# Orders of the two residuals and of the first mixer's last context state

## The reference, cut to what matters

```python
# first block
h_lat = modulate(rms_norm(lat, norm_g[i, 0]), mod_l[:, 0], mod_l[:, 1])
y_lat, y_ctx = gla_mixer(h_lat, h_ctx, ...)      # the context is scanned first, its state starts the scan of the tokens
lat = lat + (mod_l[:, 2] * rms_norm(y_lat, norm_g[i, 1])).astype(lat.dtype)              # first residual
h = modulate(rms_norm(lat, norm_g[i, 2]), mod_l[:, 3], mod_l[:, 4])
lat = lat + (mod_l[:, 5] * rms_norm(swiglu(h, ffn_w_in[i], ffn_w_out[i]), norm_g[i, 3])).astype(lat.dtype)  # second residual
# second block
h = h + 0.5 * swiglu_2(rmsnorm(h, ffn1_norm[l]), ffn1_w1[l], ffn1_w3[l], ffn1_w2[l])
```

## Time and profile before

| | us |
|---|---|
| median of 3 runs | 1572.92 (1571.53 to 1576.04) |
| profiled execution, its own time | 1573.41 |
| span of the profiled execution | 1571.6 |
| PE busy | 1554.9 (99% of the span) |
| PE weight loads busy | 1401.0 (89%) |
| DVE busy | 1099.0 (70%) |
| ACT busy | 669.4 (43%) |
| POOL busy | 118.8 (8%) |

### The profile page before, as it was taken

One profiled execution on the slowest core, in us unless ns is written; L12 is line 12 of the kernel. 1 busy time (PEld: TensorE's weight loads), 2 busy tenths in 40 slices (PEclk: granted clock), 3 DMA queues, 4 the chain that ended last, 5 costly groups with the idle time before them and its releaser, 6 DMA issues.

```text
span 1571.6 us, 23036 instructions
## 1 busy us (share of the span) xinstructions
PE 1554.9 (99%) x9758; PEld 1401.0 (89%) x9758; DVE 1099.0 (70%) x1264; ACT 669.4 (43%) x848; POOL 118.8 (8%) x106
## 2 busy tenths in 40 slices
PE   9999999999999999999999999999999999999998
PEld 7888888889999899889899889888988898998997
DVE  5898755688668567699667648646447886785675
ACT  4554275445445425445435425321223452452541
POOL 0100000020000000000000000354006000000000
PEclk9999999999999999999999999999999999999999
DMA  9544510222322322313323322333212222232231
GB/s 386 197 172 161 214 54 28 83 75 85 108 81 108 134 81 108 108 56 106 104 85 108 120 94 79 138 121 107 81 54 81 81 94 94 108 113 103 108 108 54
DMA packets 35878, 172.05 MB, mean 109 GB/s; under 512 B 3008, under 2 KB 5312, under 8 KB 26176
## 3 DMA queue, kind: packets, MB, share of 16 engines
q1 hardware_dynamic: 31424, 153.80, 27.4%
q0 software_dynamic: 4352, 16.78, 3.1%
HBM read 168.47 MB, written 2.10 MB: 109 GB/s over the span
## 4 chain that ended last, share of the span: by engine, by line
PE 82%; DVE 10%; DMA 3%; issue 2%; ACT 2%; POOL 0%; DVEq 0%; POOLq 0%; ACTq 0%; SPq 0%
PE bank L588 81%; DMA raw_pair<-in_ffn_in 3%; DVE form_slot L2548 3%; DVE sum_form L2542 1%; DVE raw_pair L2542 1%; DVE both L2495 1%; ACT form_slot L1738 1%; DVE x_form L2522 0%; DVE qd L2013 0%; DVE xT L2384 0%; ACT w_all L1407 0%; DVE hs L2506 0%; DVE y_ffn L2381 0%; DVE a_lo L2432 0%; DVE w_all L1935 0%
## 5 line engine op out<-in xcount | busy, mean ns | idle before, releaser
L588 PE MATMUL bank<-x_form,form_slot 128*128 128x256 f32 x4536 | 547.7, 283 | 3.4 <-ACT snap_a L1745 1.9
L588 PEld LDWEIGHTS bank<-x_form,form_slot 128*128 128x128 f32 x4536 | 545.9, 192 | 5.6 <-ACT snap_a L1745 2.5
L588 PE MATMUL bank<-g_slot,unit_slot 128*128 128x512 f32 (+1 forms) x1614 | 361.4, 385 | 0.0
L588 PEld LDWEIGHTS bank<-g_slot,unit_slot 128*128 128x128 f32 x1614 | 298.6, 188 | 60.1
L1738 ACT ACTIVATE form_slot<-raw_pair 128x1024 fp32r<-128x1024 f32 x135 | 140.4, 1054 | 235.2 <-PE bank L588 123.9
L588 PE MATMUL bank<-a_hi,w_all 128*128 128x512 f32 x768 | 233.8, 393 | 1.6 <-ACT a_hi L1848 0.9
L2548 DVE TENSOR_TENSOR form_slot<-raw_pair,form_slot 128x1024 fp32r<-128x1024 f32 x135 | 164.1, 1221 | 73.3 <-ACT form_slot L1738 73.2
L588 PEld LDWEIGHTS bank<-a_hi,w_all 128*128 128x128 f32 x768 | 143.1, 188 | 34.0 <-issue 3.8
L588 PE MATMUL bank<-a_lo,w_all 128*128 128x512 f32 x384 | 141.9, 390 | 0.2 <-DVE a_lo L2403 0.2
L1935 DVE TENSOR_TENSOR w_all<-w_raw,w_all 128x2048 fp32r<-128x2048 f32 x38 | 89.8, 2363 | 50.7 <-ACT w_all L1407 50.6
L1407 ACT ACTIVATE w_all<-w_raw 128x2048 fp32r<-128x2048 f32 x40 | 76.5, 1913 | 114.0 <-PE bank L588 114.0
(11 more groups left out here) (313 smaller groups left out, 1823.3 us busy)
## 6 DMA issues: line engine op xcount, KB each, us to landing
raw_pair<-in_ffn_in SPq DMA_DIRECT2D x54, 1024.0 KB, 5.1
w_raw<-in_ffn_out SPq DMA_DIRECT2D x24, 1024.0 KB, 5.0
mod_raw<-in_mod POOLq DMA_DIRECT2D x16, 1024.0 KB, 5.5
w_raw<-in_ffn_in SPq DMA_DIRECT2D x12, 1024.0 KB, 4.8
w_raw<-in_gla_in SPq DMA_DIRECT2D x10, 1024.0 KB, 5.4
w_raw<-in_mix_in SPq DMA_DIRECT2D x10, 1024.0 KB, 4.7
w_raw<-in_ffn_out SPq DMA_DIRECT2D x12, 768.0 KB, 4.2
mod_w<-in_mod SPq DMA_DIRECT2D x8, 1024.0 KB, 18.5
```

The lines of the kernel that those rows point to most:

```text
L588: return pe.matmul(out, lhs, rhs, start=first, stop=last, skip_group_check=True)
```

## The change

In the context part, PE runs `turn_keys(0)` before the last `context_state`, with two waits put ahead of it, and `mod_map(7)` moves from behind `scores(0)` to a place ahead of it. DVE copies the last context values before it splits the weight unit of slot 0, and no longer between the two splits.

In the first residual, PE drops `keep_busy(4, 2)` at the start of `gla_sums` and one of the 8 filler matmuls at its end. DVE computes the second mean square directly behind the first, scales only chunk 0 of y, makes both halves of `lo_half(1, ...)` behind it one after the other between steps of chunks 0 and 1, and scales chunks 1 and 2 later.

In the second residual, PE shortens the filler ahead of the first sum from 5 to 1, puts the last terms of two sums (`ffn_last_sums`) behind the first chunk's matmuls of unit 0 in `first_pair`, and fills with 2 and 5 matmuls elsewhere. DVE computes the product of x and y of the last chunk (`y_terms_of(1, 7)`) behind the sum of chunk 0 and no longer before the root, makes the halves of the weight split apart from each other, and computes the second mean square (`x_mean_square(1)`) behind chunk 1.

```diff
--- before.py
+++ after.py
@@ -878,9 +878,6 @@
                 values_of_pair(3)
                 context_unit(h + 1)
             mod_map(5)
-            context_state(HG - 1)
-            filled[3] = filled[4] = False
-
             def turn_keys(h):
 
                 if h:
@@ -950,13 +947,18 @@
                     m.then_inc(o_turned, 1)
 
             for h in range(HG):
+                if h == 0:
+                    pe.wait_ge(ctx_tok, cnt.upto(ctx_tok, HG))
+                    pe.wait_ge(log_gate, cnt.upto(log_gate, 16))
                 turn_keys(h)
+                if h == 0:
+                    context_state(HG - 1)
+                    filled[3] = filled[4] = False
                 r_half(h, 0)
                 if h == 0:
                     mod_map(6)
+                    mod_map(7)
                 scores(h)
-                if h == 0:
-                    mod_map(7)
                 if h == 0:
                     pe.wait_ge(free[7], cnt.next(free[7]))
                     filled[7] = False
@@ -1008,7 +1010,6 @@
 
             def gla_sums():
 
-                keep_busy(4, 2)
                 pe.wait_ge(sum_step, cnt.next(sum_step, KD - 1))
                 wide_sums(4, dec_k[2], True, False)
                 keep_busy(0, 2)
@@ -1024,16 +1025,21 @@
 
                 pe.wait_ge(y_terms, 14 + 11)
                 wide_sums(0, dec_k[0], True, False)
-                keep_busy(3, 5)
+                keep_busy(3, 1)
                 pe.wait_ge(pair_out[1], cnt.now(pair_out[1]))
                 wide_sums(0, tmp[0], False, True).then_inc(sums_ready, 1)
                 pe.wait_ge(y_terms, 14 + 12)
                 wide_sums(6, dec_k[1], True, False)
-                pe.wait_ge(y_mixed, cnt.next(y_mixed, 2 * (KD - 1)))
-                wide_sums(6, tmp[1], False, True)
+                keep_busy(3, 2)
                 spread_roots(5, 0)
                 pe.wait_ge(sum_step, cnt.next(sum_step, KD - 1))
                 wide_sums(4, dec_k[2], True, False)
+                keep_busy(3, 5)
+
+            def ffn_last_sums():
+
+                pe.wait_ge(y_mixed, cnt.next(y_mixed, 2 * (KD - 1)))
+                wide_sums(6, tmp[1], False, True)
                 pe.wait_ge(y_squared, 3 * KD)
                 wide_sums(4, tmp[2], False, True).then_inc(sums_ready, 1)
 
@@ -1053,6 +1059,8 @@
                         m = mm(bank[2 * u + c][:], weights(u, k, c)[0], a_lo[:, k], False, k == KD - 1)
                         if k == KD - 1:
                             m.then_inc((silu_in, up_ready)[u], 1)
+                    if roots_at is not None and (u, k) == (0, 0):
+                        ffn_last_sums()
                     if (u, k) == roots_at:
                         spread_roots(4, 2 * PAIRS, roots_spread)
                 filled[0] = filled[1] = filled[2] = filled[3] = False
@@ -1060,7 +1068,7 @@
             gla_sums()
             keep_busy(3, 3)
             spread_roots(4, PAIRS)
-            keep_busy(0, 8)
+            keep_busy(0, 7)
 
             def ffn(f, up_after=None):
 
@@ -2215,8 +2223,8 @@
             middle_parts(0)
             less_middle(1)
             mod_parts(11, 14)
+            context_values(3)
             split_lo(0)
-            context_values(3)
             split_lo(1)
             context_state_out(3)
 
@@ -2350,17 +2358,14 @@
                 if half:
                     m.then_inc(lo_done[s], 1)
 
-            def residual_roots(n):
+            def y_root(n):
 
                 dve.wait_ge(sums_ready, cnt.next(sums_ready))
                 V.tensor_scalar(col4[:, 0:PAIRS], wide((6, 0)[n]), 1.0 / D, EPS, ALU.mult, ALU.add).then_inc(var_done, 1)
-                lo_half(1, 0)
-                if n:
-                    lo_half(1, 1)
+
+            def x_mean_square(n):
+
                 dve.wait_ge(root_done, cnt.next(root_done))
-                if n:
-                    dve.wait_ge(roots_ready, cnt.next(roots_ready))
-                    y_by_root(1, 0)
                 dve.wait_ge(sums_ready, cnt.next(sums_ready))
                 q, r = ssq[:, 0:PAIRS], root4[:, 0:PAIRS]
                 before = x_var[:] if n == 0 else col4[:, PAIRS:2 * PAIRS]
@@ -2372,8 +2377,6 @@
                 V.tensor_tensor(q, q, r, ALU.mult).then_inc(dve_step, 1)
                 dve.wait_ge(dve_step, cnt.next(dve_step))
                 V.scalar_tensor_tensor(col4[:, c0:c0 + PAIRS], q, 1.0 / D, before, ALU.mult, ALU.add).then_inc(var_done, 1)
-                if n == 0:
-                    dve.wait_ge(roots_ready, cnt.next(roots_ready))
 
             def y_by_root(n, m):
 
@@ -2390,9 +2393,11 @@
                     y_terms_of(0, m, (y_squared, 2 * m + 1), 2 * m + 2)
                 if n < 3:
                     split_lo(n % 2)
-            residual_roots(0)
-            for m in range(3):
-                y_by_root(0, m)
+            y_root(0)
+            x_mean_square(0)
+            dve.wait_ge(roots_ready, cnt.next(roots_ready))
+            y_by_root(0, 0)
+            lo_half(1, 0)
             dve.wait_ge(root_done, cnt.next(root_done))
             dve.wait_ge(roots_ready, cnt.next(roots_ready))
 
@@ -2413,9 +2418,11 @@
                 cnt.expect(scaled)
 
             norm_mod(0)
+            y_by_root(0, 1)
+            lo_half(1, 1)
+            lower_mod(0)
             norm_mod(1)
-            lower_mod(0)
-            lo_half(1, 1)
+            y_by_root(0, 2)
             lower_mod(1)
             y_by_root(0, 3)
             for m in range(2, KD):
@@ -2731,7 +2738,7 @@
                         split_lo(0)
                     if f == 0:
                         y_terms_at(CPU * p)
-                        if p != 2:
+                        if p < 2:
                             y_terms_at(CPU * p + 1)
                     elif f == 1 and p < 3:
                         x_lower(CPU * p, next_gains)
@@ -2739,13 +2746,21 @@
 
             ffn(0)
 
-            residual_roots(1)
+            y_root(1)
+            lo_half(1, 0)
+            dve.wait_ge(roots_ready, cnt.next(roots_ready))
+            y_by_root(1, 0)
+            cnt.expect(pair_out[1])
+            y_terms_of(1, KD - 1, None, None)
             x_lower(0, lambda m: col("ffn1_g", m))
+            lo_half(1, 1)
             y_by_root(1, 1)
             for m in range(2, KD + 1):
                 if m < KD:
                     y_by_root(1, m)
                 x_lower(m - 1, lambda m: col("ffn1_g", m))
+                if m == 2:
+                    x_mean_square(1)
             dve.wait_ge(root_done, cnt.next(root_done))
             ffn(1, lambda m: col("ffn1_g", m), lambda m: col("mix_g", m))
             for m in (6, 7):
```

## The result

The changed kernel takes 1576.35 us (median of 20 runs, 1573.27 to 1578.51), the kernel before, beside it on the same chip, 1572.49 us (20 runs, 1570.53 to 1576.04). The ratio is 1.0024, 95% interval 1.0018 to 1.0031: 3.8 us slower, 2.8 to 4.9. That is inside "within 0.3%" and inside the range, but three times the +1.2 us of the forecast, and beyond the 3 us that the forecast itself had named as a sign of being wrong. Three of the 99 executions of before that stand beside the experiments, 1692, 1694 and 4249 us long, are left out everywhere. The profiled execution took 1575.64 us (span 1573.8), 2.2 us more than that of before. So there are two questions: whether the 2.2 us in the traces lie where the forecast put them, and where the timed runs got 1.6 us more.

What follows compares the result with a forecast made beforehand. PE was taken as the bound behind the first residual and DVE behind the second. Context +0.1, first residual +0.3 and second +0.76 sum to +1.2 us, forecasting a median of 1574.1 us, range 1570.8 to 1576.8.

Steps and rivals of the forecast that it cites:

- within 0.3%: Whole kernel: the time stays within 0.3% of before (4.7 us), chance 0.92; faster 0.04, slower 0.04.
- forecast 1.6: Context part: the clock falls behind the thin stretch, leaving 3.2 us of PE's work at half rate, 1.6 us lost.
- -1.5 at full clock: Context part: at full clock 1.5 us are won of the 3.1 by which the gate matmuls start earlier.
- forecast +0.3: First residual: the split for the second group ends 0.3 us too late for PE; ends -0.65 and +0.7.
- DVE's delay: First residual: DVE is 1.1 us later, and so is the split for the second group.
- forecast +0.76: Second residual: DVE, and with it PE at the split, comes 0.76 us later; ends +0.2 and +1.1.
- The product (0.60): Second residual: chunk 7's product of x and y, in an idle time before, adds 0.60 us to DVE's list.
- the wait (0.27): Second residual: DVE waits for ACT's `a_hi` after the sum of chunk 0, +0.27 us.
- the clock holds: Rival, context part: no clock fall at the two maps, so -1.5 there, -0.4 in all, 1572.5 us; chance 0.22.
- the change doesn't do what it says: Rival, context state: PE waits for another semaphore, the 3.1 us are not won, 1575.6 us at most; chance 0.05.
- absorbed and kept: Rival, residuals: DVE's delay absorbed, first residual's lead kept; -2.0, 1570.9 us with the clock holding, 1572.5 with a fall; chance 0.13.
- fall in the residuals: Rival, residuals: the clock falls there, 1.7 us lost in each; 4.6 us in all, 1577.5 us; chance 0.08.

Runs made afterwards that it cites:

- fill_wait: The changed kernel with 8 filler matmuls, behind the wait for banks 0 and 1, ahead of `mod_map(7)`: 1575.81 us, ratio 1.0019 to before.
- res1_only: The kernel before with only the first residual's part of the change: 1573.06 us, ratio 1.0002 to before.
- res2_only: The kernel before with only the second residual's part of the change: 1573.77 us, ratio 1.0002 to before.
- y1_first: The kernel before with the first residual's part, chunk 1 of y scaled directly behind chunk 0, ahead of the first half split: 1573.72 us, ratio 1.0003 to before.
- before_fill: The kernel before with 5 filler matmuls in its wait at the last context state, order unchanged: 1572.48 us, ratio 0.9999 to before.
- map7_behind: The changed kernel with `mod_map(7)` back behind `scores(0)`: 1572.62 us, ratio 0.9999 to before.
- ctx_map7_behind: The kernel before with the context part of the change, but `mod_map(7)` left behind `scores(0)`: 1571.98 us, ratio 0.9991 to before.
- best_again: The kernel before with the context part but `mod_map(7)` left behind `scores(0)`, timed again on another chip: 1571.07 us, ratio 0.9991 to before.
- ctx_only: The kernel before with only the context part of the change: 1574.12 us, ratio 1.0007 to before.
- terms_back: The changed kernel with the last chunk's product of x and y back ahead of the roots in the second residual: 1575.40 us, ratio 1.0017 to before.
- half_in_wait: The changed kernel with the last chunk's product back ahead of the roots and the second half split ahead of the first `a_lo`: 1576.09 us, ratio 1.0022 to before.
- after: The profiled execution of the changed kernel, all parts of the change against the kernel before: 1575.64 us.
- after_again: The changed kernel unaltered, timed again on another chip: 1575.85 us, ratio 1.0023 to before.

## Why the forecast was right in kind and short in size

**The clock, and what the pair of traces hides.** Against the trace of before, the context part came out as forecast: +0.1 us at the second head's `turn_keys` (205.99 against 205.56, less 0.33 by which the execution was late at 12 us already), with its wait of 1.98 us (forecast 1.9), a fall of 3.4 us and a loss of 1.71 (forecast 1.6). The forecast weighed a rule of the Trainium skill (TensorE: Matmul & The Clock Gate, Part 1: The HAM clock gate), that idleness drops the clock and not thin matmuls. The runs agree with it: in fill_wait the same two maps, with the wait filled, have no fall behind them. But the -1.5 us that the forecast gave the rule did not come, since all five traces with the wait of 2.0 us unfilled have a fall.

The step that failed is the term "-1.5 at full clock". It compares a context part without a fall with a trace of before that has one, and so counts 1.7 us of clock as won. Without the clock the table's column "O less it" is 315.4 to 315.8 for the old order (before, res1_only, res2_only, y1_first, before_fill) and 315.1 to 316.1 for the new one. Counted from the transposes near 118.5 the means are 197.06 and 197.10: 0.0 us, where removed and added waits cancel. What remains is how often the clock falls, and that the timed runs tell. The five runs with another order or filled waits, whose traces have no fall in mid-kernel (map7_behind, ctx_map7_behind, best_again, fill_wait, before_fill), have mean granted clocks of 0.9985 to 0.9987; before has 0.9979, 0.9982 and 0.9984 on three chips, the changed kernel 0.9970 and 0.9973. The others fit: 0.9981 to 0.9984 for the three with the old order (res1_only, res2_only, y1_first), 0.9970 to 0.9976 for the three with the new one (ctx_only, terms_back, half_in_wait). Times 1575 us, before lacks some 0.6 us against them and the changed kernel 2.2. With 1.71 us for one fall (3.41 for a double one) that is one in about every third execution of before, and more than one in each of the changed kernel. The profiled pair showed 1.71 in both. This is an estimate, since each run's clock is given to three digits only and holds the half clock of the last 10 us too (a shortfall of 1.1 to 2.7 us in the traces); three of the four traces with the old order unfilled do have the fall. It puts the clock's part at +1.7 us, and ctx_only's +1.1 (-0.3 to +2.7) agrees. So does before by itself: its 32 runs at 0.999 took 1572.2 us in the mean, its 64 at 0.998 or 0.997 took 1573.6. fill_wait does not: its clock is as high as that of the five, yet it is 3.0 us slower than before (1.6 to 4.4), where the terms without a fall give 1.1 (0.0 + 1.05 + 0.67, less before's 0.6).

**The first residual**: forecast +0.3, measured +1.05 (O to M in after, after_again and map7_behind). The mechanism was as described (a lead at unit 1, stalls of 0.24 and 0.25 us at chunks 1 and 2, a late split for the second group), but DVE is 1.55 us later there (349.34 - 317.77 against 347.36 - 317.35) and not 1.1. The term that was too small is DVE's delay: the third `norm_mod` comes 0.5 us later than the 332.0 forecast (332.97, less 0.42 for the later O), and the wait of 0.50 us for POOL ahead of the second one is just that. POOL's sum was priced at its unhindered 1.27 us and took 2.19 beside the split. As the split ended 0.8 us ahead of PE before, PE waits for all that is more: it takes the unit 34.00 us behind O and not 33.09, 0.9 us later where the forecast had 0.3. y1_first shows that starting POOL earlier doesn't mend it; no run kept POOL's sum and the half splits apart, so that their contention is the cause is read from the traces and not tested.

**The second residual**: forecast +0.76, measured +0.67, with the wrong terms. The product (0.60) and the wait (0.27) were added up, but the product lies in the wait. What costs is that DVE waits for `a_hi` with nothing ready ahead of it, since both the second half split and the mean square (0.8 us, which filled this very time before) moved behind:

```profile
680.95 0.16 DVE L2368 TENSOR_TENSOR ssq<-bank,root 128x4 f32<-128x4 f32 x1
...
681.72 0.75 DVE L2432 SCALAR_TENSOR_TENSOR a_lo<-xT,cols,a_hi 128x512 fp32r<-128x512 f32 x1
```

In these rows of before the first `a_lo` follows the mean square with no wait. That the sum came out right was luck: the wait that the product left uncovered is about as long as the product and the forecast's wait together. half_in_wait shows it.

**Sum.** 0.0 (context without the clock) + 1.7 (clock, an estimate) + 1.05 + 0.67 = 3.4 us, against 3.8 (2.8 to 4.9) measured. Of this, that the place of `mod_map(7)` decides between 3.8 us and nothing is shown by map7_behind; how its share divides into clock and wait is read from the traces. In the profiled pair it is 0.1 + 1.05 + 0.67 and the 0.33 at the start, 2.15 of 2.2. Of the rivals, "the clock holds" and "the change doesn't do what it says" fell with the trace, and so did "absorbed and kept": `hs` came 2.12 us later and nothing behind gave it back. The clock did not fall in the residuals either. What the rivals lacked is a slower one at the old place: falls in the context part, which by the mean clocks most executions of before do without. The range holds 1576.35 with 0.45 us to spare, by a width that was taken from the scatter of the runs and not from these terms.

**Open.** Why fill_wait, with the clock of a kernel without a fall, is no faster than after_again (0 +/- 1.5 us). If what its one trace lost behind O against after's (0.57 us up to M, 1.03 behind `hs`), with late transfers in sight, came in most executions, that would close the gap; no run shows how often it does, and whether the fillers themselves cost something was not tested. half_in_wait, 0.9 us better at one mark, shows no gain in its median either, but there the sum of the terms, 2.6 us above before, lies within what was measured (2.0 to 4.9).

## What to carry to other kernels

A clock fall in one profile may be a matter of chance: ask of the timed runs' mean granted clocks how often it comes, before counting it as won or lost. Move a consumer ahead of other work only if its input is ready: one map put ahead of the scores cost a wait, with a fall of the clock behind it in every trace, and putting it back won all of the 3.8 us. An instruction taken off an engine's list is worth nothing if the next one waits for another engine just as long; look first for what fills that wait.

## What the runs showed of the hardware

- The half clock in mid-kernel came in pieces of one size: a shortfall of 1.70 or 1.71 us in seven traces, and 3.41 in one.
- The same code with the same wait of 1.2 us (before, res1_only, res2_only, y1_first) had the fall in three traces and not in one. With 2.0 us of waiting, unfilled, it came in all five; with fillers in either wait (fill_wait, before_fill) in neither of two, and in none of the three with neither wait (map7_behind, ctx_map7_behind, best_again).
- Contention of POOL and DVE goes with what DVE does: POOL's sum of 128x512 took 2.18 to 2.20 us beside a half split, which uses no bank, and 1.27 to 1.30 beside work that reads or writes a bank; in y1_first the split itself went from 1.22 to 1.64 us. POOL's 2.19 us are about the 0.97 from its start (327.33) to DVE's next instruction behind the split (328.30) and then its usual 1.27. The Trainium skill (GPSIMD Engine Reference, 1. Specifications) says that GpSimd shares its SBUF interfaces with VectorE and that VectorE instructions with two SBUF inputs contend for them; the split has two such inputs, and the traces agree. The forecast didn't draw on it.
